# A hybrid decoder step on one core: the tokens in two groups, the second group's path laid between the expert gathers of the first

## The chip, the core and the metric

The kernel runs on one core of a Trainium2 chip. All tensors are 32-bit floats. The metric is the device time of one execution in microseconds (us). A core has five engines, each with its own instruction queue that is worked off strictly in order: TensorE (PE, matrix products into PSUM), VectorE (DVE), ScalarE (ACT), GpSimd (POOL) and SyncE (SP). Engines wait for each other through semaphores. DMA transfers are issued here by POOL (the "software" queue) and by SP (the "hardware" queue), and are carried by the core's 16 DMA engines.

## What is computed

One layer for 512 prompt tokens and 8 sample tokens of width 1024. Cut to what matters:

```python
ada = silu(c) @ w_ada + b_ada                      # six vectors of 1024 for the prompt, six for each sample
h = rmsnorm(x, g_pre_mix) * (1 + sc1) + sh1
aq, ak, av, conv_in, a_dec, b_beta, z, g_a, g_b = split(h @ w_in)
o_att = sliding-window attention (window 128, 8 heads, 2 key/value heads, sinks, relative bias)
conv_out = silu(4-tap causal convolution of conv_in)          # 1536 channels
o_d = gated delta rule over chunks (recurrent state, 4 heads of 128x128), RMS norm, gate silu(z)
merged = sigmoid(g_a) * (o_att @ w_att_out) + sigmoid(g_b) * (o_d @ w_delta_out)
x = x + gt1 * rmsnorm(merged @ w_out, g_post_mix)
h2 = rmsnorm(x, g_pre_ffn) * (1 + sc2) + sh2
# expert retrieval, for every token and each of 8 heads:
s = (h2 @ w_query) against 2 x 128 sub-keys;  16 best of each half, 16 best of their 256 sums
u, v = expert_u[eidx], expert_v[eidx]              # 16 experts a head, rows of 1024 each
f = sum over experts of softmax(best) * gelu(h2 . u) * v
x = x + gt2 * rmsnorm(f, g_post_ffn)
```

Besides x it returns the last keys and values, the last convolution inputs and the recurrent state of both token sets. Attention and delta rule look back only: a token needs the 128 keys before it, the 3 convolution inputs before it and the state left by earlier chunks.

## The kernel before, in words

**Two parts.** The first part (the "front") takes all 520 tokens through everything up to the scores. The second part is the expert retrieval. For tiles of 128 tokens (t = 0, 1, 2, the 8 samples as t = 4, then t = 3) and 8 heads (a "unit" is one tile and head) it gathers expert rows: one indirect DMA brings 128 rows of 8 KB (u and v side by side, 1 MB) into one of 7 ring slots. 4 gathers are a "quad", 4 quads a unit, 520 gathers in all.

**The loop per gather** (loops over QUADS on POOL, ACT, PE and DVE). POOL issues gather n (L338) when PE has freed slot n % 7 (ring_used). DVE takes the dot product of the slot's u half with the replicated tokens (L1427, dots_done). ACT applies gelu (L540) and scales the selection pattern S (L547, diag_ready). PE multiplies S with the v half, twice 512 columns, into fsum[0] and fsum[1] (L952 for tiles, L955 for the samples) and frees the slot. Before, each gather has its two products in turn: fsum[0], then fsum[1]. Between them DVE works on `search` for the unit two ahead, PE and ACT on `select` and, at the start of each tile, `replicate`. For t = 0 a quad also takes one block of w_query for tiles 1 to 3 and the samples (`query`).

**The front** in PE's order: 16 blocks of w_ada (`modulation`), transposes of x, 12 projections for the convolution, keys and values (wnat), 4 for the queries, 8 norms with projections between them, 4 attention blocks of 128 tokens with 3 projections each, the samples' attention, the delta rule (transposes, decay matrices, `lv` 1 to 6 of a triangular solve, recurrence over 4 chunks, the samples' step), 8 branch projections, `mix` with w_out for 5 tiles, `residual` on DVE, 16 query blocks for tile 0. `project` takes one 512 KB weight block with 8 products for each of two column parts (256 and 264 tokens). The profile records each 32-bit product as two entries. Almost all matrix products go through `mm` (L588). Weight blocks come on SP's queue in stream order into 4 or 5 places; SP waits for `w_used` of the block that held the place. POOL's queue carries all other loads and stores, and later the gathers.

**Order.** It is written out by hand, the same on every engine. PSUM: 4 banks that DVE empties (dbank), 2 that ACT empties (abank), 2 for fsum.

## Time and profile before

| | us |
|---|---|
| median of 3 runs | 2160.33 (2159.97 to 2164.02) |
| the profiled execution, its own time | 2168.11 |
| its span, first to last instruction | 2166.3 |
| first gather issued | 784.2 |
| mean granted TensorE clock | 0.940 of full |

| engine | busy us | share of the span |
|---|---|---|
| PE | 1681.8 | 78% |
| DVE | 1274.2 | 59% |
| ACT | 593.5 | 27% |
| POOL | 640.9 | 30% |

The profile is of one execution. Its page divides the span into 40 slices of some 54 us and shows each engine's busy share in tenths, the granted clock and the DMA traffic. The chain of waits is followed back from the last instruction. Shares over the whole span hide that the two parts have different limits, so the stretches before and after 784 us must be read apart.

### The profile page before, as it was taken

What the parts mean: (1) busy time and instruction counts of PE and PEld (TensorE: products, weight loads), DVE (VectorE), ACT (ScalarE), POOL (GpSimd) and SP (SyncE); (2) the same over time, 40 slices, a digit from 0 to 9 for tenths busy, and PEclk for the clock granted to TensorE, in tenths of its full rate; (3) what the DMA queues carried; (4) which work ended last, traced back from release to release, by engine and by line L of the source; (5) the groups of instructions that cost most, each with busy time, mean ns of one, the idle gap of its engine ahead of it and who ended that gap; (6) DMA issues with size and microseconds to landing.
All of it is one profiled execution on the core that took longest, in us unless ns stands there. A gap on an engine that the chain in (4) does not pass through costs nothing.

```text
span 2166.3 us, 22269 instructions
## 1 busy us (share of the span) xinstructions
PE 1681.8 (78%) x7458; PEld 810.0 (37%) x7458; DVE 1274.2 (59%) x2848; ACT 593.5 (27%) x1653; POOL 640.9 (30%) x596
## 2 busy tenths in 40 slices
PE   4999898979699988786776766776766777677776
PEld 1776677769676463332111111111111111111111
DVE  3441432177553655556666766767666767766754
ACT  1122344312100132223224223224223224332222
POOL 1001000000000024333544544544444543544542
PEclk9999999979789999998998999998999999899999
DMA  8336541000015179999999999999999998999997
GB/s 283 127 111 187 145 139 49 30 1 1 6 53 222 47 272 402 403 388 371 419 414 390 421 412 421 418 419 385 421 413 413 416 413 358 401 421 421 421 422 305
DMA packets 97954, 636.83 MB, mean 294 GB/s; under 512 B 11489, under 2 KB 11521, under 8 KB 30716
## 3 DMA queue, kind: packets, MB, share of 16 engines
q0 software_dynamic: 79248, 564.07, 64.4%
q1 hardware_dynamic: 18592, 71.34, 9.5%
q8 instruction: 59, 0.97, 0.2%
q14 instruction: 55, 0.45, 0.1%
HBM read 628.85 MB, written 7.56 MB: 294 GB/s over the span
## 4 chain that ended last, share of the span: by engine, by line
PE 43%; DMA 31%; ACT 10%; DVE 9%; issue 5%; another core or an unknown queue 1%; POOL 1%; ACTq 0%; DVEq 0%; SPq 0%; POOLq 0%
DMA arena<-in_euv,delta 28%; PE abank L588 18%; PE fsum L952 11%; PE dbank L588 9%; DVE arena L1427 3%; DMA arena<-in_wstream 2%; ACT delta L547 2%; ACT L492 1%; ACT L540 1%; ACT arena L352 1%; ACT small L540 1%; PE abank L905 1%; PE abank L891 1%; DVE arena L1174 1%
## 5 line engine op out<-in xcount | busy, mean ns | idle before, releaser
L952 PE MATMUL fsum<-arena,delta 128*32 128x512 f32 x2048 | 831.2, 673 | 369.3 <-ACT delta L547 367.4
L1427 DVE CUSTOM_DVE_ANT_0 arena<-arena 128x1024 f32<-128x1024 f32 x520 | 635.1, 1223 | 446.0 <-DMA arena<-in_euv,delta 430.7
L338 POOL DMA_INDIRECT arena<-in_euv,delta x520 | 595.7, 1146 | 735.4 <-PE fsum L952 648.2
L952 PEld LDWEIGHTS fsum<-arena,delta 128*32 128x32 f32 x2048 | 183.2, 118 | 970.5 <-ACT delta L547 669.0
L588 PE MATMUL abank<-arena 128*128 128x256 f32 (+5 forms) x2080 | 447.7, 375 | 23.0 <-DMA arena<-in_wstream 8.5
L588 PEld LDWEIGHTS abank<-arena 128*128 128x128 f32 (+2 forms) x2080 | 350.5, 191 | 122.1 <-issue 29.5
L540 ACT ACTIVATE small<-small 128x1 f32<-128x1 f32 x520 | 103.9, 200 | 641.3 <-DVE small L1427 627.9
L588 PE MATMUL dbank<-arena 128*128 128x128 f32 (+9 forms) x1072 | 225.9, 373 | 8.0 <-ACTq L461 2.9
L352 ACT ACTIVATE arena<-abank 128x512 f32<-128x512 f32 (+4 forms) x202 | 101.3, 501 | 415.1 <-PE abank L588 382.3
L588 PEld LDWEIGHTS dbank<-arena 128*128 128x128 f32 (+3 forms) x1072 | 165.1, 205 | 66.8 <-issue 50.1
L547 ACT ACTIVATE delta<-arena,small 128x32 f32<-128x32 f32 (+1 forms) x520 | 166.9, 321 | 17.2 <-ACT small L540 0.2
L309 POOL DMA_DIRECT2D out_deltap<-delta x1 | 0.6, 550 | 280.3 <-DVEq L1216 280.3
L1093 DVE RECIPROCAL arena<-arena 128x520 f32<-128x520 f32 x8 | 27.2, 3403 | 63.4 <-ACTq L408 63.4
L328 POOL CAST delta<-delta 128x16 uint32<-128x16 f32 x32 | 21.2, 662 | 131.1 <-ACTq L500 130.9
L623 PE MATMUL dbank<-arena,cT 128*9 128x256 f32 x384 | 34.6, 459 | 22.6 <-DMA arena<-in_wstream 16.3
L540 ACT ACT_TABLE_LOAD x35 | 44.9, 1283 | 0.8 <-ACT arena L352 0.2
L1427 DVE DVE_READ_ACCUMULATOR2_ANT small<- 128x1 f32 x520 | 42.7, 82 | 0.0
L492 ACT ACT_TABLE_LOAD x32 | 41.1, 1283 | 2.5 <-DVE arena L1360 0.6
L477 ACT ACTIVATE small<-small 128x1 f32<-128x1 f32 (+1 forms) x15 | 4.4, 294 | 129.7 <-DVE small L1283 129.6
L553 ACT ACTIVATE arena<-abank 128x384 f32<-128x384 f32 x16 | 7.9, 491 | 109.9 <-PE abank L588 109.9
L352 ACT ACTIVATE delta<-abank 128x32 f32<-128x32 f32 (+1 forms) x33 | 6.5, 197 | 113.6 <-PE abank L891 82.1
L905 PE MATMUL abank<-arena,consts 128*32 128x512 f32 x256 | 35.3, 602 | 1.8 <-ACT arena L352 1.8
(262 smaller groups left out, 1099.7 us busy)
## 6 DMA issues: line engine op xcount, KB each, us to landing
arena<-in_wstream SPq DMA_DIRECT2D x124, 512.0 KB, 4.6
arena<-in_euv,delta POOLq DMA_INDIRECT x520
arena<-in_x POOLq DMA_DIRECT2D x2, 2048.0 KB, 19.7
arena<-in_wout SPq DMA_DIRECT2D x1, 4096.0 KB, 17.3
arena<-in_sdel POOLq DMA_DIRECT2D x1, 2048.0 KB, 9.0
out_deltas<-arena POOLq DMA_DIRECT2D x1, 2048.0 KB, 8.7
arena<-mod POOLq DMA_DIRECT2D x4, 512.0 KB, 17.0
out_yp<-arena SPq DMA_DIRECT2D x4, 512.0 KB
```

Of the source, the lines that this page charges most:

```text
L338: pool.indirect_dma_start(ring[n % SLOTS], None, I["euv"], bass.IndirectOffsetOnAxis(cur[:, u % 2, c:c + 1], 0)).then_inc(ring_in[n % SLOT ...
L352: step(A(dst, src, func, **kw), s.aring_free)
L492: A(gexp[r, :], best[r, :], ACT.Exp, bias=nbest[r, :], accum_out=gsum[r, :]).then_inc(s.gexp_ready, 1)
L540: step(A(gel[:, q % 2, j:j + 1], dot[:, q % 2, j:j + 1], ACT.Gelu), s.gelu_done)
L547: A(S[:, q % 2, j, 0:wide], E4g[:, u % 2, c0:c0 + wide], ACT.Copy, scale=gel[:, q % 2, j:j + 1]).then_inc(s.diag_ready, 1)
L588: return pe.matmul(out, lhsT, rhs, start=first, stop=last)
L623: last = pe.matmul(mod_bank[0][32 * j:32 * j + NCOND, half * 256:half * 256 + 256], cT[:, at_, :], w[:, j * 256:(j + 1) * 256], start=at_ ...
L891: last = pe.matmul(b[32 * k:32 * k + 32, 8 * j:8 * j + 8], ident[:, 32 * j:32 * j + 32], pick[:, :, 4 * k:4 * k + 4], start=True, stop=Tru ...
L905: last = pe.matmul(b[32 * k:32 * k + 32, :], ident[:, 32 * j:32 * j + 32], h2[:, t, g * 512:(g + 1) * 512], start=True, stop=True, skip_gr ...
L952: last = pe.matmul(fsum[g][32 * j:32 * j + 32, :], S[:, q % 2, j, :], v, start=first_quad(q), stop=last_quad(q), skip_group_check=True)
L1093: step(recip(r, r))
L1427: TTR(uh, uh, rep[j] if t < NT else h2sb, 1.0, 0.0, ALU.mult, ALU.add, dot[:, q % 2, j:j + 1]).then_inc(s.dots_done, 1)
```

## The change

The tokens are cut in two groups: group 0 is tokens 0 to 255, group 1 is tokens 256 to 511 and the 8 samples. On PE, ACT and DVE the front becomes a Python generator `group(g)` that yields after each of many short segments, 281 in all (118 of group 0, 163 of group 1); a segment has the same number on all three engines. Before the retrieval starts, 110 segments are issued: all of group 0 up to its 9th of 16 query blocks. The retrieval is cut in "ticks" of 2 gathers (8 a unit, 4 for the samples), and after each tick the engine issues its segments up to a due number:

```diff
+SEGS_BEFORE = 110
+SEGS_ALL = 281
+PACE = 1.55
+def due(i):
+    if i < 0:
+        return SEGS_BEFORE
+    return min(SEGS_ALL, SEGS_BEFORE + int((i + 1) * PACE))
```

PE issues up to due(i) after tick i, ACT and DVE up to due(i - 1). So the 171 remaining segments lie in the first 111 or so of 260 ticks. Tile 2's search needs group 1's scores from tick 112 on.

The weight stream has the blocks of w_in after w_ada, the branches and w_query a second time (60 blocks of 512 KB), and w_out is loaded twice, in halves; group 1 has 4 places of its own:

```diff
+    order += list(range(QUERY, QUERY + 16))
+    first = len(order)
+    order += list(range(CONV, QUERY + 16))
...
+PLACE = [n % 5 if n < N_EARLY else 5 + (n - N_EARLY) % 4 for n in range(len(STREAM))]
```

`project` has one part (256 or 264 columns). Group 1's loads and stores (x, the caches, bias, the samples' state, w_out, the modulation rows) are issued by SP in between, each behind a wait; POOL has only gathers from the first one on. Group 1's w_out and weights share memory, so the second half of w_out waits for three results of the first, and the query weights for all six:

```diff
+            sp.wait_ge(s.merged_ready, N.merged_ready + KT)
+            sp.dma_start(wout[1][0], I["wout"][:, :, 0:512]).then_inc(s.wout_in, 16)
...
+            sp.wait_ge(s.mx_ready, N.mx_ready + 3)
+            sp.dma_start(wout[1][1], I["wout"][:, :, 512:D]).then_inc(s.wout_in, 16)
+            sp.wait_ge(s.mx_ready, N.mx_ready + 6)
```

Carried from group 0 to group 1: the last 3 convolution inputs (`carry`), the last 128 keys and values (`kvc`), the state (`delta`).

In the retrieval loop on PE the two gathers of a tick are taken together, first both into fsum[0], then both into fsum[1]; their S patterns have different groups of 32 output rows:

```diff
+                pair = [(n + e, (2 * (k % 2) + e)) for e in range(2)]
+                for e in range(2):
+                    for n_, j in pair:
+                        if e == 0:
+                            pe.wait_ge(s.diag_ready, n_ + 1)
+                        v = ring[n_ % SLOTS][:, D + 512 * e:D + 512 * e + 512]
...
+                            last = pe.matmul(fsum[e][32 * j:32 * j + 32, :], S[:, n_ // NQ % 2, j, :], v,
...
+                n += 2
+                if k == 0 and u + 1 < len(UNITS):
+                    select(u + 1)
...
+                work.until(due(i))
```

PSUM: 2 banks for `select` and `replicate` alone (fbank), 4 for the front (2 that DVE empties, 2 that ACT empties; group 0 borrows the fsum banks for DVE's). Group 0's solve has one gate projection a level, its recurrence two, each attention block two; group 1's 16 gate projections stand in a row after the samples' state. In the convolution ACT now makes the first tap, and DVE the other three as one instruction each for the prompt; the samples' taps are 8 instructions for all 12 blocks. `mix` goes to banks that ACT empties. The window copies of the caches are issued near the start.

## Rows read from the trace of the kernel before

**Rows 1.** The page's 40 slices, DMA busy share and rate.

```profile
DMA  8336541000015179999999999999999998999997
GB/s 283 127 111 187 145 139 49 30 1 1 6 53 222 47 272 402 403 388 371 419 414 390 421 412 421 418 419 385 421 413 413 416 413 358 401 421 421 421 422 305
```

**Rows 2.** Windows: busy us of PE, PEld, DVE, ACT, POOL; clock, DMA share, GB/s.

```profile
0.00:784.20 784.20, 690.02 (x3752) 533.11 (x3753) 357.85 (x631) 172.32 (x348) 23.53 (x44) 0.94 0.32 104
784.20:2166.30 1382.10, 991.74 (x3712) 276.94 (x3708) 916.39 (x2218) 421.14 (x1305) 617.42 (x552) 0.94 0.98 402
...
850.00:900.00 50.00, 40.81 (x205) 18.55 (x198) 30.27 (x78) 13.13 (x45) 20.08 (x19) 0.97 0.99 402
...
1900.00:1950.00 50.00, 36.60 (x114) 7.83 (x113) 34.86 (x87) 16.61 (x49) 24.46 (x22) 1.00 1.01 422
```

**Rows 3.** The gathers' line: duration ns min/median/max, starts; POOL's idle time before.

```profile
L338 POOL DMA_INDIRECT arena<-in_euv,delta x520: 939/947/4372, 784.2 to 2140.3; - x174
...
  PE fsum L952: 648.2, 310
```

**Rows 4.** Timeline: the first gather's dot; one gather of the steady part, DVE to PE.

```profile
789.84 1.23 DVE L1427 CUSTOM_DVE_ANT_0 arena<-arena 128x1024 f32<-128x1024 f32 x1 [3.79 <-DMA arena<-in_euv,delta]
...
1930.08 1.23 DVE L1427 CUSTOM_DVE_ANT_0 arena<-arena 128x1024 f32<-128x1024 f32 x1 [1.25 <-DMA arena<-in_euv,delta]
...
1931.34 0.20 ACT L540 ACTIVATE small<-small 128x1 f32<-128x1 f32 x1 [1.93 <-DVE small L1427]
1931.58 0.32 ACT L547 ACTIVATE delta<-arena,small 128x32 f32<-128x32 f32 x1
...
1931.95 1.91 PE L952 MATMUL fsum<-arena,delta 128*32 128x512 f32 x4 [0.58 <-ACT delta L547]
```

**Rows 5.** Chain that ended last: start us, us; a backlogged quad and a gather.

```profile
837.32 3.99 PE fsum L952 x16
...
1930.16 12.21 DMA arena<-in_euv,delta
```

**Rows 6.** The same chain through the front, where its stages begin.

```profile
54.95 8.97 PE abank L588 x32
...
149.84 25.31 PE abank L588 x112
...
204.56 7.27 PE abank L588 x32
...
213.63 19.65 DMA arena<-in_wstream
...
312.63 8.76 PE abank L588 x48
...
426.30 6.01 PE dbank L588 x34
...
480.77 1.16 PE abank L588 x8
...
547.20 1.17 PE abank L588 x8
...
589.12 14.22 PE dbank L588 x66
...
606.98 67.01 PE dbank L588 x272
...
675.30 69.03 PE dbank L588 x160
...
746.34 7.43 PE abank L588 x64
```

**Rows 7.** DMA issues: KB each, us from issue to landing.

```profile
skew<-bext POOLq DMA_DIRECT2D x1, 1536.0 KB, 37.0
```

**Rows 8.** Groups of instructions by line: busy us, mean ns, idle before.

```profile
L540 ACT ACT_TABLE_LOAD x35 | 44.9, 1283 | 0.8 <-ACT arena L352 0.2
L1093 DVE RECIPROCAL arena<-arena 128x520 f32<-128x520 f32 x8 | 27.2, 3403 | 63.4 <-ACTq L408 63.4
```

2303 lines of the change are left out of this document (1351 added, 952 removed).

## The prediction, made before the result was known

> **What bounds the kernel now.** I read the page's slices first. The DMA row is low and ragged up to slice 14 and stands at 9 from there to the end, at 370 to 422 GB/s [rows 1]. So there are two parts with different limits. The windows put numbers to them: from 0 to 784.2 us the DMA engines are busy 0.32 of the time and PE for 690 us; from 784.2 on DMA is busy 0.98 of 1382.1 us, PE 992, DVE 916 [rows 2]. The gathers' own line dates the border: 520 of them, first issued at 784.2, and POOL sits idle 648 us before them, released by PE freeing a slot [rows 3]. That could look like a bound by PE, but a gather takes 12.21 us from issue to landing [rows 5], and at 422 GB/s [rows 2] one MB takes 1.049/0.422 = 2.49 us, so some five are in flight: the slots are the limit on what is queued, DMA on the rate. The work on a landed gather is short: dot 1.23, gelu 0.20, S 0.32, products 1.91 us, about 3.8 us in all [rows 4]. 7 slots x 2.49 = 17.4 us is one round of the ring; without its DMA part 12.2 about 5 are left, and they are used. The second part is thus bound by bytes (545 MB of gathers / 0.422 = 1292 us of its 1382), the first by PE's order and the cross-engine chains.
>
> **The change, the part before the first gather.** Only group 0 goes ahead. A projection of all tokens takes 7.27 us [rows 6]; with 256 columns 3.6. Stage by stage, from the starts in [rows 6]: up to 54.95 nothing is per token, 55 us stay 55. Convolution 94.9 us for 12 blocks, 7.9 each, becomes 4.3 each: 51. Keys, values, queries 54.7: two tiles of five and four narrower projections: 29. Norms 108.1, with a 19.65 us wait for weights which falls together with the skewed write, 37.0 us to landing [rows 7], which stays: less 8 x 3.6 and a little, 75. Attention 113.7 for four blocks: two blocks and fewer projections in them, but the softmax chain stays whole: 50. Samples' attention and decay matrices 54.5: 20. Solve 66.4, 11.1 a level: half the DVE work, but a projection of 3.6 on PE is put in each level: 63. Recurrence 41.9: two chunks, two projections: 28. Samples' step 17.9: gone. Branches 68.3: 29. Mix 71.0: 4 of its 10 sums, 28, and the last tile's residual no longer hidden by mix, 12: 40. Queries 37.9: 9 blocks of 3.6, scores, search, select: 39. The sum is 479; I take a first gather at **480**, bounds 445 and 535 (the lower if the weight wait goes, the upper if norms and attention are chains and keep their length). Against 784.2 that is **-304 us** (-339 to -249).
>
> **The change, the bytes that come in.** While gathers run, group 1 brings 60 weight blocks (31.5 MB), 7 of group 0 (3.7), w_out 4.2, x twice 2.1, wnat 1.1, bias 1.0, caches 1.0, state in and out 4.2, modulation rows 1.6: 50.4 MB, where the kernel before had 16 blocks, 8.4 MB. 42 MB more at 0.402 to 0.422 [rows 2] is **+100 to +105 us, I take +103**. That a weight block costs no more than its bytes is shown at 850 to 900, where one block a quad came in at 0.99 DMA share [rows 2].
>
> **The change, what the weave costs beyond bytes.** 171 segments at 1.55 a tick are 110 ticks. Their DMA time is 110 x 4.97 = 547 plus 50.4/0.422 = 119: 666 us, 6.05 a tick. DVE's own retrieval work is 34.86 of 50 us [rows 2], 3.45 a tick, 381 us; group 1 adds about 175 (half of 357.85 [rows 2], less a convolution that is cut to three instructions, plus the samples): 556. PE: a lone gather costs 1.91 [rows 4], a backlogged one 3.99/4 = 1.0 [rows 5], since products of different gathers write different rows of a bank and overlap when they are neighbours in the queue; the new pairing makes them neighbours, so 220 x 1.0 = 220. Group 1's and group 0's last products are some 420: 67 projections of 3.6 are 240, mix 6 x 6.9 = 41 (69.03 for 10 [rows 6]), the rest is half of what 690 leaves. 640 in all. So PE and DVE both fit under 666 **on average**. They don't fit in each stage, and here I price what goes beyond the bytes. The rule: DVE does the segments one tick later than PE. Of two segments in a tick the second waits on PE for the first one's answer, which DVE gives only behind its next dots. For a stage with DVE work d a segment and an answer of p from PE and ACT, a tick is about 3.45 + 1.55 d + 0.55 p.
> - Solve, 14 segments, 9 ticks: DVE 4.3 a level (half the 8.6 or so of four chunks), then dots, ACT, PE: some 11 us a level or 8.4 a tick against 5.0: +31.
> - Residual of three tiles: 24 us DVE on top of 20 in 6 ticks, six roots that each need a table load of 1.28 [rows 8]: 53 against 29, +24.
> - Mix: 41 + 7 us PE in 4 ticks plus two waits for halves of w_out behind the gathers' traffic: +25.
> - Recurrence +19, decay matrices +15, norms (a reciprocal of half of 3.4 [rows 8] and a table load each) +15, attention +14 with the wait for bias, samples' attention and step +19, waits for x and state +10, the rest +10.
> Sum +182. A stall of up to 12.2 - 5.6 = 6.6 us costs nothing when five gathers are in flight (5.6 is the first gather, alone in the queue, from its issue at 784.2 [rows 3] to its dot at 789.84 [rows 4]), four or so times: -27. I take **+155**, bounds 0 (averages decide) and +300 (each of the 171 segments waits 1.75 us more, near the 1.91 of a lone product [rows 4]).
>
> More DVE work could also slow POOL. A gather's issue takes 947 ns in the median and 4372 at most [rows 3], so something blocks it at times. Of this SBUF — State Buffer of the Trainium skill (Who interferes with whom) says that GpSimd cannot write descriptors while DVE runs a copy or tensor_scalar in a two-port mode, while a tensor_tensor with two inputs does not stop it. Group 1's DVE work is nearly all of the second kind, so by the rule nothing is added; were it of the first, 1 us on each of 220 issues would still lie under the 3 us that a gather has.
>
> A table load shows 1283 ns, with 0.8 us of idle time before all 35 of a group [rows 8]. ScalarE: Activation LUTs of the Trainium skill (What ACT_TABLE_LOAD costs) counts a drain with each switch, 2.66 us in all. Some 30 visits to another table, there and back, are 77 us of ACT by the row and 160 by the skill; the sum goes by the row.
>
> **The sum.** Span 2166.3 - 304 + 103 + 155 = 2120. The profiled execution lies 1.8 above its span and 7.8 above the median of the runs: 2120 + 1.8 - 7.8 = **2114 us**. After tick 111 the parts are alike, and the end is the same.
>
> **Rivals.**
> 1. *The weave hides nearly everything* (mechanism: the ring's cushion and three engines that run a tick apart absorb the stage peaks; DMA stays at 9). For it: at 850 to 900 PE was at 40.81 of 50 us and DMA still at 0.99 [rows 2]. Against: that work had no chain in it. It costs 40 instead of 155: about 2000 us (1960 to 2050).
> 2. *The weave locks the engines in step*, and the gathers starve: place, the chain stages (norms to recurrence, mix, residual); each wait on PE holds back the products that free slots, POOL issues late, and after five landed gathers DMA runs dry. It decides from a loss of 304 - 103 = 201 us, or a tick of (666 + 201)/110 = 7.9 us. With 1.75 us more a segment the loss is 300: about 2260 (2170 to 2320). For it: PE has 640 of 666 us of work, so nothing of what it waits is given back, and POOL is released by PE in 648 us of its waits [rows 3]. Against: only some 100 segments have a chain.
> 3. *The front does not shrink as said*, since it is chains and not columns: first gather at 535, the rest as forecast: 2169, slower by a hair or the same.
>
> **Chances.** Forecast (2050 to 2165) 0.43, rival 1 0.26, rival 2 0.25, rival 3 0.06. The range that leaves out 2 in 10 reaches into both main rivals: 1985 to 2220. The cases of both signs hold much of the chance; the likeliest one's own range is 2050 to 2165. A measurement tells 0.2% (4.3 us) from no change. Faster by more: 0.26 + 0.39 = 0.65; within: 0.05; slower: 0.25 and parts of rival 3 and of the forecast's upper end, 0.30.
>
> **What the profile after would show.** Front: the first gather at 480, and 11 us a level of group 0's solve. Bytes: 42 MB more in all, DMA share 0.9 or less from 480 to about 1300 with dips at solve, mix and residual, 0.98 or more afterwards. Weave: the gather of tick 111 issued some 820 us after the first (666 + 155) against 547 by bytes alone; rival 1 has it at 710, rival 2 at 960. Pairing: products of a tick in about 2 us. If POOL's idle time is released by products that themselves waited for DVE or ACT in segments, rival 2's mechanism is at work. It would be wrong in size if loads on SP's queue landed late enough to hold PE for more than a few us each, or if PE's granted clock fell in its waits.

## The result, and the profile after it

The changed kernel takes **2242.24 us** (median of 4 runs, 2232.38 to 2246.39) beside 2160.47 for the kernel before: 1.0368 times as long, 95% interval 1.033 to 1.0407. It is slower by 3.7%. The forecast was 2114, faster, with 2220 as its upper end: wrong in sign, and outside its range. The profiled execution has a span of 2230.6 us.

The page's 40 slices of the kernel after, 56 us each, to be read beside [rows 1]:

```profile
PE   3968687879498668886698567966766666666664
DMA  7766023139799779684699557899999999999997
GB/s 270 236 168 221 19 73 126 57 103 356 285 375 351 275 295 354 236 302 192 265 377 369 206 216 272 348 412 394 407 421 421 421 420 367 377 421 421 421 421 301
```

Gathers run from the end of slice 9 on. Up to slice 26 the DMA row goes up and down between 4 and 9, and GB/s between 192 and 377; from slice 27 on both stand as they did before. The changed kernel has three parts: the front (up to the first gather), the weave (the stretch in which segments and gathers alternate, up to the gather of tick 111), and a rest that is like the old one. Windows of the kernel after (columns as in [rows 2]):

```profile
0.00:495.60 495.60, 373.44 (x2018) 282.07 (x2022) 163.18 (x296) 110.54 (x208) 13.11 (x26) 0.90 0.44 140
495.60:1438.90 943.30, 721.11 (x3485) 401.29 (x3478) 563.77 (x1278) 326.42 (x821) 251.33 (x235) 0.85 0.78 299
1438.90:2230.60 791.70, 506.67 (x1983) 109.32 (x1981) 527.01 (x1257) 242.05 (x744) 374.12 (x317) 0.94 0.97 400
```

And before, the stretch in which the same 222 gathers were issued, from the first one to that of tick 111:

```profile
784.20:1375.90 591.70, 436.14 (x1776) 145.16 (x1772) 383.71 (x946) 181.80 (x567) 258.85 (x235) 0.93 0.98 401
```

The gathers' own line after, and what ended POOL's idle time ahead of it, beside [rows 3]:

```profile
L358 POOL DMA_INDIRECT arena<-in_euv,arena x520: 939/947/1999, 495.6 to 2205.8; - x174
...
  PE fsum L1202: 968.4, 258
```

So the first gather comes 288.6 us sooner (784.2 to 495.6), the weave takes 351.6 us more (591.7 to 943.3), and the last 298 gathers keep their 2.57 us each. -288.6 + 351.6 = +63, which is the difference of the two profiled spans (64.3). All that is to be explained lies in those 943 us. On average no engine is full in them: PE is busy 721 us, DVE 564, DMA 0.78. The change would have paid below 591.7 + 288.6 = **880 us**.

What the weave looks like from near, in windows of 50 us: a stretch of projections, one with w_out, and one with the residual:

```profile
1100.00:1150.00 50.00, 50.00 (x249) 32.86 (x248) 19.49 (x43) 13.64 (x43) 14.30 (x15) 1.00 0.88 349
1250.00:1300.00 50.00, 35.93 (x130) 12.27 (x131) 2.62 (x10) 5.39 (x17) 5.67 (x6) 0.86 0.41 150
1300.00:1350.00 50.00, 19.52 (x49) 5.41 (x45) 33.11 (x59) 21.21 (x39) 13.39 (x11) 0.61 0.68 262
```

PE is full in the first, idle for 14 of 50 us in the second with DVE all but stopped, and idle for 30 in the third at a granted clock of 0.61. Each stage has another limit. The chain of waits names them. First a wait for the samples' x, then PE in front of the two halves of w_out (SP asks for each only when group 1 has come far enough; the profile names no releaser there and says "issue", and that it is w_out is shown by e5 below), then the residual:

```profile
554.58 12.79 DMA arena<-in_xs
...
1220.35 1.84 PE fsum L1202 x8
1222.19 15.84 issue
1238.03 16.34 PE bank L751 x32
...
1263.42 14.07 issue
1277.49 15.39 PE bank L751 x32
...
1316.11 1.28 ACT L601
...
1317.93 1.30 DVE arena L1703
1319.25 1.24 DVE arena L1704
...
1325.41 1.28 ACT L601
...
1327.23 1.30 DVE arena L1694
...
1334.70 1.28 ACT L601
```

The 1.28 us before each root (square root on ACT) is a table load, and the roots follow one another 9.3 us apart, one a tick: between them lie DVE's sums, two dots, another table load for gelu, S, and only then the next root.

To compare runs I use two numbers of each: the length of the weave (first gather to that of tick 111) and PE's busy time in it. PE's waits are the difference. And I divide the weave by stages, at the starts of the dots whose ticks carry them. "Forecast" is what the prediction listed for the stage beyond its average tick. In the changed kernel:

```text
stage of group 1              ticks     from-to, us      us a tick  over 6.05 a tick   forecast
x, norm, transposes           0-10      503.3-591.2        8.8        +27                +10 (x and state)
convolution to g/beta         10-26     591.2-707.8        7.3        +20   )
gates, branches               70-86    1066.0-1206.6       8.8        +44   )            +10 (the rest)
h2 transposes to scores       96-110   1344.9-1442.9       7.0        +13   )
norms                         26-32     707.8-765.8        9.7        +22                +15
attention                     32-42     765.8-837.8        7.2        +12                +14
decay matrices                47-51     866.5-895.0        7.1         +4                +15
solve                         51-59     895.0-960.1        8.1        +17                +31
recurrence                    59-64     960.1-997.9        7.6         +8                +19
samples' attention and step   42-47, 64-70                 8.8        +30                +19
mix and residual              86-96    1206.6-1344.9      13.8        +78                +49
sum                                                                  +275               +182
```

The borders are those of DVE, which runs ahead of PE, so a stage of PE can show late. This matters in the last row. DVE's dots of tick 91 start at 1237.0 us and those of tick 92 at 1303.6: before its first residual part DVE waits for all six sums of `mix`, and PE needs from 1222.2 to 1301.6 us for them, 29.9 us of it in the two waits. The six ticks with a root each (92 to 97) take 8.9, 9.3, 9.3, 13.8, 9.3 and 7.4 us, 58 in all, the fourth with a 3.67 us wait for modulation rows.

### The profile page after: what moved, and what is told of

Same layout as the page of the kernel before. It is cut to its first block, busy times and chain, and to the rows that moved or that the text cites. A ratio compares the mean times of both kernels' runs of the same rounds, so it can differ in the third digit from the quotient of the medians.

```text
span 2230.6 us, 22523 instructions
## 1 busy us (share of the span) xinstructions
PE 1601.2 (72%) x7480; PEld 792.7 (36%) x7480; DVE 1254.0 (56%) x2830; ACT 679.0 (30%) x1772; POOL 638.6 (29%) x578
## 2 busy tenths in 40 slices
DMA packets 112212, 667.87 MB, mean 299 GB/s; under 512 B 12353, under 2 KB 15953, under 8 KB 44972
## 4 chain that ended last, share of the span: by engine, by line
PE 39%; DMA 25%; DVE 18%; issue 9%; ACT 8%; DVEq 0%; SPq 0%; POOL 0%; ACTq 0%; POOLq 0%
PE bank L751 26%; DMA arena<-in_euv,arena 20%; PE fsum L1202 9%; DVE arena L1867 5%; DMA arena<-in_wstream 4%; PE fsum L751 1%; ACT arena L727 1%; ACT small L720 1%; PE fbank L1183 1%; DVE arena L1547 1%; PE bank L819 1%; DVE arena L1451 1%; ACT arena L387 1%; DVE arena L1563 1%; PE fsum L776 1%
## 5 line engine op out<-in xcount | busy, mean ns | idle before, releaser
L1202 PE MATMUL fsum<-arena 128*32 128x512 f32 x2048 | 725.8, 674 | 350.4 <-ACT arena L727 348.0
L358 POOL DMA_INDIRECT arena<-in_euv,arena x520 | 607.3, 1168 | 1086.1 <-PE fsum L1202 968.4
L751 PE MATMUL bank<-arena 128*128 128x264 f32 (+9 forms) x2960 | 679.2, 388 | 113.9 <-DMA arena<-in_wstream 31.5
L751 PEld LDWEIGHTS bank<-arena 128*128 128x128 f32 (+4 forms) x2960 | 520.1, 200 | 292.0 <-issue 132.7
L1202 PEld LDWEIGHTS fsum<-arena 128*32 128x32 f32 x2048 | 134.3, 116 | 846.7 <-ACT arena L727 632.3
L387 ACT ACTIVATE arena<-bank 128x512 f32<-128x512 f32 (+3 forms) x150 | 77.1, 514 | 419.0 <-PE bank L751 403.1
L727 ACT ACTIVATE arena<-arena,small 128x32 f32<-128x32 f32 (+1 forms) x520 | 166.9, 321 | 18.1 <-ACT small L720 0.6
L720 ACT ACT_TABLE_LOAD x59 | 75.7, 1283 | 66.2 <-DVE small L1867 64.1
L819 PE MATMUL bank<-consts,arena 128*128 128x128 f32 x176 | 32.7, 338 | 54.6 <-DVE arena L1479 29.3
L1402 DVE SCALAR_TENSOR_TENSOR arena<-arena,cols 128x256 f32<-128x256 f32 x72 | 35.1, 487 | 60.0 <-ACT arena L424 58.3
L1183 PE MATMUL fbank<-arena,consts 128*32 128x512 f32 x256 | 37.7, 652 | 5.0 <-ACT arena L672 5.0
## 6 DMA issues: line engine op xcount, KB each, us to landing
arena<-in_sdel SPq DMA_DIRECT2D x1, 2048.0 KB, 11.9
```

The source lines that it names most:

```text
L358: pool.indirect_dma_start(ring[n % SLOTS], None, I["euv"], bass.IndirectOffsetOnAxis(cur[:, u % 2, c:c + 1], 0)).then_inc(ring_in[n % SLOT ...
L387: step(A(dst, src, func, **kw), s.aring_free)
L720: step(A(gel[:, q % 2, j:j + 1], dot[:, q % 2, j:j + 1], ACT.Gelu), s.gelu_done)
L727: A(S[:, q % 2, j, 0:wide], E4g[:, u % 2, c0:c0 + wide], ACT.Copy, scale=gel[:, q % 2, j:j + 1]).then_inc(s.diag_ready, 1)
L751: return pe.matmul(out, lhsT, rhs, start=first, stop=last)
L819: last = pe.transpose(b[:, e * P:(e + 1) * P], src, ident)
```

## The experiments

All times are medians, each with the kernel before run beside it (2160 to 2168 us). "Weave" and "busy" are from the profiled execution.

```text
kernel                   time us   ratio to before (95%)       weave   PE busy   PE waits  clock  DMA
changed                  2242.24   1.0368 [1.033, 1.0407]       943     721       222      0.85   0.78
e1_unpaired              2237.76   1.0359 [1.034, 1.0377]       946     721       225      0.86   0.78
e3_pace3                 2350.18   1.087  [1.0852, 1.0889]     1057     766       291      0.85   0.69
e5_no_wout               2216.56   1.0239 [1.0216, 1.0262]      913     715       198      0.87   0.80
e6b_no_loads             2189.78   1.0102 [1.0078, 1.0127]      894     719       175      0.87   0.79
e7_no_sqrt               2231.14   1.0301 [1.0281, 1.0321]      941     721       219      0.86   0.78
e8_no_lag                2565.36   1.1832 [1.1801, 1.1863]     1258     832       426      0.80   0.60
e9_by_gather             2340.27   1.0802 [1.078, 1.0825]      1044     827       217      0.88   0.73
e10_dve_later            2229.12   1.0286 [1.0266, 1.0306]      928     716       212      0.85   0.79
e11_after_5places        2408.01   1.1111 [1.1088, 1.1134]      994     747       247      0.84   0.75
e12_few_bytes            2249.11   1.0384 [1.0363, 1.0405]      951     727       224      0.84   0.72
e13_two_ticks            2316.24   1.0678 [1.0648, 1.0708]     1024     744       280      0.83   0.73
e14_by_weight            2236.87   1.0327 [1.0304, 1.035]       938     726       212      0.87   0.79
e15_best                 2218.99   1.0239 [1.0213, 1.0265]      916     725       192      0.87   0.80
e16_half_projections     2217.19   1.0238 [1.0216, 1.026]       918     656       262      0.83   0.78
e17_half_products        2209.00   1.0198 [1.0179, 1.0216]      913     643       270      0.81   0.79
e18_all_three            2161.54   0.9978 [0.9962, 0.9994]      868     578       290      0.77   0.76
```

### The pairing (e1_unpaired, e2_before_paired)

```diff
-                for e in range(2):
-                    for n_, j in pair:
+                for n_, j in pair:
+                    for e in range(2):
```

> The changed kernel with one part undone: PE takes the two gathers of a tick one after the other again (fsum[0], fsum[1], then the next gather). If PE's own work is what fills the weave (640 of some 666 us by the prediction), a tick's products go from about 1.85 us to about 2.6 us where PE is behind, over 111 ticks 80 us, and the time rises to about 2320. If the weave is long because engines wait for each other and for loads, PE has idle time in most stages and only the projection stages (some 55 ticks) feel it: 20 to 45 us, about 2275.

> The kernel before with the pairing alone: in a quad the products of gathers 0 and 1 are taken together, then those of 2 and 3. DMA bounds its second part, so all theories expect little: 0 to -8 us, the gain only in tile 0 where queries load PE. A loss of up to 15 us would show that holding back a slot until its neighbour's pattern is there costs the ring more than PE gains.

e1 gives 2237.76 and the same weave; e2, the kernel before with pairs, 2168.01 us (ratio 1.0022, 1.0007 to 1.0037), no gain and perhaps a hair slower. Both of e1's expected values are missed: the order within a pair is without weight. It is another question whether two gathers side by side cost less than two set apart; e9 shows below that they do.

### What group 1's path costs by itself (e4_unwoven, e3_pace3)

e4 issues group 1's path up to segment 258 before the first gather:

```diff
-SEGS_BEFORE = 110
+SEGS_BEFORE = 258
...
-    if i < 0:
+    if i < 50:
         return SEGS_BEFORE
-    return min(SEGS_ALL, SEGS_BEFORE + int((i + 1) * PACE))
+    return min(SEGS_ALL, SEGS_BEFORE + int((i - 49) * PACE))
```

> The changed kernel with 258 segments before the first gather: all of group 1 up to its first query blocks runs without gathers in between, only the last 23 segments are woven in, from tick 50 on. It measures group 1's path alone. From group 0's own path (443 us from its convolution to the first gather) I expect 380 to 430 us for it, the first gather at 880 to 930, and about 2290 in all. What the weave hides is that length less the 350 us by which the woven ticks are longer than the same ticks before: 30 to 80 us. If contention between gathers and the weave's loads were the cause of the long ticks, the path alone would be short, 300 us, and this kernel would be faster than the woven one, near 2190.

2447.25 us, ratio 1.1329 [1.1305, 1.1352]. The window over what was put ahead, and the 222 gathers after it:

```profile
495.60:1062.70 567.10, 387.95 (x1801) 296.78 (x1803) 184.18 (x340) 104.42 (x226) 0.20 (x1) 0.80 0.23 75
1062.70:1656.00 593.30, 414.00 (x1756) 123.60 (x1748) 392.38 (x979) 187.88 (x573) 279.06 (x235) 0.93 0.98 400
```

This is the number that my forecast never worked out. Two groups one after the other take 1062.7 us to where one pass over all tokens took 784.2: 278.5 more. PE's busy time accounts for 76 of it (378 + 388 against 690), its idle time for the other 203: it goes with what comes twice, the chains, the table loads and the waits for transfers, which I haven't priced one by one. My expectation for e4, 380 to 430 us for this path, was far too low as well, and its rival, that gathers and loads hinder each other and the path alone is short (300 us), is refuted. What lies ahead of the gathers in e4 and not in the changed kernel is 567 us, PE busy in 388 of them: group 0's last queries and group 1's path up to the transposes of h2. The last 23 segments are woven from tick 50 on and cost nothing (593.3 for 222 gathers), as the 16 whole query blocks cost nothing in the kernel before. The weave hides 567 - 351.6 = 215 us of this, 38%. It would have had to hide 279.

e3 sets the rate to 3.0 segments a tick instead of 1.55, so that 57 ticks carry them.

> The changed kernel with a pace of 3.0 segments a tick instead of 1.55: the weave takes 57 ticks instead of 111. If every segment has a price of its own (chains through three engines, waits for loads), the weave's segments cost the same and fewer gathers are hidden under them: the 57 ticks take about 57 x 13 = 740 us, the other 54 then 280, 1020 against 943: about 2320. If the price is one of ticks (each handshake of a tick costs once) the time falls, to about 2150 to 2200. If bytes bound it, the sum of bytes is the same and the time stays at 2242.

The 57 ticks took 759 us, the weave 1057, the whole 2350.18: near the numbers expected of "each segment has its own price". Fewer ticks beside the segments hide less.

### Waits for group 1's loads (e5_no_wout, e6b_no_loads) and roots (e7_no_sqrt)

e5 leaves out both loads of w_out of group 1 and their waits, e6b also those of x, skew, caches, state and modulation rows:

```diff
-            sp.dma_start(wout[1][0], I["wout"][:, :, 0:512]).then_inc(s.wout_in, 16)
...
-            sp.dma_start(wout[1][1], I["wout"][:, :, 512:D]).then_inc(s.wout_in, 16)
```

> The changed kernel without the second group's two loads of w_out (2 x 2.1 MB): the mixing product of group 1 reads what already lies in those areas, so its values are not the reference's. In the changed kernel the tensor engine waits 15.84 us and 14.07 us for the two halves, each asked for by SP only after a step of group 1. Theory 'the lateness is made of waits for loads that are asked for too late': the two waits go, and nothing else moves in, 2197 to 2212 us (30 to 45 less than 2242). Rival 'it is the bytes': 4.2 MB at 421 GB/s are 10 us, 2232 us. Rival 'something else is late there anyway': 2242 us.

> The changed kernel without group 1's own loads of x, skew (the attention's bias), the samples' keys and values, the samples' state (sdel), w_out and the modulation rows: group 1 computes on what already lies in those places, so its values are not the reference's. The weight stream, the natural weights and the residual's x stay. Some 12 MB are not moved, 29 us of bytes. Theory 'waits for loads asked for at the last moment': the waits of 21 (x), 9.6 (skew), 11.9 (state), 15.8 and 14.1 us (w_out) and 3.7 (modulation) go, the time falls by 75 to 100 us to 2142 to 2167, which is the time before or a little under. Rival 'bytes alone': 2213. Rival 'the engines run in each other's step, waits for loads lie beside that': over 2213.

> The changed kernel with each of group 1's square roots on ScalarE (the norm of x, the norms of keys and queries, of the delta output, of the residual) replaced by a plain copy, which needs no other function table, so its values are not the reference's. 59 table loads took 75.7 us of ScalarE in all in the changed kernel. Theory 'handshakes between ScalarE and VectorE set the pace in the stages with roots' (norms 9.7 us per tick, residual 19.4 us per tick): each load of 1.28 us and what hangs on it goes, some 15 to 30 loads of group 1 in the chain, 2202 to 2222 us. Rival 'the roots lie beside other waits': within 5 us of 2242.

e5: 2216.56 us (26 less); the weave is 30.0 us shorter, which is just the two waits of 15.84 and 14.07. Ticks 90 to 95 go from 117 to 85 us, no other stage moves by more than 3. e6b: 2189.78, the weave 49.6 us shorter: 38 in ticks 90 to 95 (to 78), 10 in the stage of x, 5 in the samples' step, while others are a little longer. PE's waits fall by 47, its busy time by 2. So waits for loads that are asked for too late are real and add one for one, but they are 50 us and not the 75 to 100 that I expected; with them gone the kernel is still 1% slower than before. e7: 27 table loads fewer, 37 us less busy time of ACT. In the ticks with roots the loads are in the chain, and there their removal shows, 7.14 us from root to root where it was 9.30:

```profile
1324.01 0.10 ACT small L611
...
1331.15 0.10 ACT small L611
```

Over the whole weave the profiled execution is only 2.5 us shorter, since other stages took longer, attention above all (6.5 us). The median is 11 lower, with single runs from 2221.72 to 2242.28 beside 2232.38 to 2246.39. So the table loads are worth some 11 us at most, between the two expectations; outside the residual the roots lie mostly beside other waits.

### The bytes (e12_few_bytes)

```diff
+                if n >= N_FIRST:
+                    sp.dma_start(wplace[PLACE[n]][:, 0:P], I["wstream"][STREAM[n]][:, 0, :]).then_inc(w_full[PLACE[n]], 16)
```

> The changed kernel, but of each of group 1's 60 weight blocks only an eighth is loaded (the same 60 transfers, waits and products; what lies in the other seven eighths of a place is used as it is, so the values are not the reference's). 27.5 MB less, 65 us at 421 GB/s. Theory of the forecast, that a byte moved in the weave costs its time at the full rate: the time falls by 65 us, to 2177. Rival 'the queue stands idle a fifth of the weave, so the bytes lie in time that is lost anyway': under 25 us, 2217 to 2242.

2249.11 us, none of the 65. 27.5 MB less brought nothing at all: the DMA share of the weave fell from 0.78 to 0.72 and its length stayed.

```profile
498.00:1448.90 950.90, 726.68 (x3485) 404.87 (x3478) 563.60 (x1278) 326.00 (x821) 247.92 (x235) 0.84 0.72 268
```

For these bytes, 65 of the 103 us that the forecast charged, the price is thereby refuted; the other bytes were not taken out by themselves. In all stages but one the DMA share is 0.94 or less. The branches alone have 0.99, with PE busy 54.3 of 56.3 us, and e12 did not shorten them either.

### The order of the engines (e8_no_lag, e10_dve_later, e11_after_5places)

In the changed kernel ACT and DVE take a tick's segments one tick after PE. e8 takes this away, e10 adds half a tick for DVE:

```diff
-                work.until(due(i - 1))
+                work.until(due(i))
...
-                work.until(due(i - 1))
+                work.until(due(i))
```

> The changed kernel, but ScalarE and VectorE take group 1's segments of a tick in the same tick as the tensor engine does, not one tick later. Theory 'each engine's part of a stage waits a whole tick for its turn': where a stage of group 1 is a ping-pong between engines it gets shorter by up to a tick in some 15 places, 2140 to 2200 us. Rival 'the lag is what lets the engines run past each other': without it ScalarE and VectorE stand waiting for the tensor engine's results ahead of the dots of group 0, slower, 2260 to 2320 us. I hold the second for likelier (0.6).

> The changed kernel, but VectorE takes group 1's segments of tick i after the first of the two dots of tick i+2, half a tick later than in the changed kernel; ScalarE stays one tick behind. Theory 'more lag, more slack between the engines' (no lag at all cost 323 us): faster, 2190 to 2225 us. Rival 'the tensor engine now waits longer for VectorE inside a tick, with the next gathers' products behind the wait': slower, 2260 to 2320 us. Even odds.

e8 gave the largest change of the study: 2565.36 us, 323 more, well past what either theory had. PE's waits, first the kernel after, then e8 (PE line, what it waited for: us, times, longest):

```profile
PE fsum L1202 <- ACT arena L727: 81.2, 24, 17.0
PE bank L751 <- issue: 29.9, 2, 15.8
PE bank L751 <- DMA arena<-in_wstream: 14.9, 1, 14.9
```

```profile
PE fsum L1202 <- ACT arena L727: 378.9, 108, 15.4
```

Without the lag the products of nearly every tick wait for ACT's S. The chain of e8 in group 1's solve shows one such tick from end to end:

```profile
1100.06 1.11 issue
1101.17 0.10 DVE small L1867
1101.29 0.21 ACT small L720
1101.53 0.33 ACT arena L727
1101.86 0.04 issue
1101.90 4.13 PE fsum L1202 x8
1106.03 3.89 PE bank L751 x32
1109.96 0.04 issue
1110.01 0.70 DVE arena L1563
```

Dot, gelu, S, products, group 1's products, group 1's DVE work, dot: one after the other, two pipelines made into one chain. This is engines in each other's step in its pure form; the lag of a tick saves 315 of the weave's us. Of these, 204 are waits of PE and 111 are busy time for the same work: the granted clock of the weave was 0.80 in e8 against 0.85, and the 8 entries of the chain above take 4.13 us at a granted clock of 0.59 where the changed kernel had 1.84 at 1.00. With half a tick more for DVE the weave is another 15 shorter (e10, 2229.12 us, ratio 1.0286, outside both of its expected ranges), PE's waits for S 62 us instead of 81; the ticks with roots go from 9.3 to 6.9 us, the norms' from 9.7 to 8.0, while solve, attention and queries get longer by 0.5 to 1.0.

> The changed kernel with 5 places for gathered rows instead of 7. A gather takes 12.2 us to land and some 4 us more to be used, so where nothing else holds it up 5 places give one per 3.2 us instead of 2.58: the stretch after the weave grows from 767 to about 960 us. The weave has 4.25 us per gather. Theory 'the weave is limited by group 1's chains and loads': it grows by under 20 us, since 16.2 us / 4.25 us are under 4 places. Rival 'a late segment is made up out of the places that wait filled': with fewer of them the weave grows by 100 us or more.

2408.01 us. The stretch after the weave took 894 us for its 298 gathers (3.0 each; 960 expected). The weave grew by 51, between the two numbers: slack in the ring helps there, but its limit is elsewhere.

### The grain of the weave (e9_by_gather, e13_two_ticks, e14_by_weight, e15_best)

e9 weaves after each gather instead of after two, with ACT and DVE two gathers behind, e13 after each fourth (cuts from PE's loop):

```diff
+                            if n_ % 2 == 0:
+                                work.until(due2(n_))
```

```diff
-                work.until(due(i))
+                if i % 2 == 1:
+                    work.until(due(i))
```

> The changed kernel, woven by the gather instead of by the tick: after each gather's product the tensor engine takes 0 or 1 segment of group 1 (0.775 on average; by the tick it was 1 or 2), and ScalarE and VectorE take theirs two gathers behind it, which is the same lag. Same segments, same total. Taking the lag away cost 323 us, so the order in the tick has weight. Theory 'the engines run in each other's step, a tick at a time': in smaller portions a gather's product is held up by one segment rather than two, and the weave shrinks by 30 to 80 us, 2160 to 2210 us in all. Rival 'it is the segments' own chains': the same 2242 within 8 us.

> The changed kernel, woven by two ticks: the tensor engine issues group 1's segments only after every second tick, 3 or 4 at once, ScalarE and VectorE one tick later. Four gathers' products stand next to each other. Theory 'the tensor engine's own work is the limit, and products that stand alone cost nearly twice' (272 us for 216 gathers' products in the weave, 379 us when woven by the gather, with 100 us more in the time): products at 1.0 us a gather, 216 to 225 us in the weave, some 50 us less, 2180 to 2205 us in all. Rival 'the chains of group 1 weigh more': three dependent segments in a portion each wait a hand-over, so the chain stages (norms, attention, residual) grow as the products shrink, 2240 to 2320 us. I give the first 0.45.

Both went the other way: e9 2340.27 us, e13 2316.24. e9's reason stands in its chain, here in the stage of gates:

```profile
1183.67 1.83 PE fsum L1209 x4
1185.50 3.76 PE bank L758 x16
```

4 entries, one gather, take 1.83 us; in the changed kernel 8 entries, two gathers, take 1.84 (the chain above, at 1220.35). The products of two gathers go to different groups of 32 rows and run together if they are neighbours in the queue. Apart they cost PE double where PE is full; over the weave it is busy 105 us more and the weave is 100 longer. PE's lines over the weave, gathers' products only, the kernel after and e9 (busy us, mean ns, then idle before):

```profile
L1202 PE MATMUL fsum<-arena 128*32 128x512 f32 x864 | 271.7, 696 | 82.5 <-ACT arena L727 81.2 <-ACT arena L387 0.7
```

```profile
L1209 PE MATMUL fsum<-arena 128*32 128x512 f32 x864 | 379.0, 665 | 125.6 <-ACT arena L734 125.5
```

e13 had the reverse: its products did not get cheaper (294 us), and PE waited 170 us for S instead of 81. My reading, for which I show no chain: with three or four of group 1's segments in a row, each needing an answer that DVE and ACT give only after their next dots, PE comes late to the next tick. My theory for e13, that joining four gathers makes their products cheaper and the time shorter, fell here. One tick is the best of the three grains.

e14 gives stages of projections 2.1 to 2.6 segments a tick, chain stages 0.8 to 1.35:

```diff
-    return min(SEGS_ALL, SEGS_BEFORE + int((i + 1) * PACE))
+    at = float(SEGS_BEFORE)
+    for _ in range(i + 1):
+        at += next((r for end, r in RATES if at < end - 1e-6), 1.0)
+    return min(SEGS_ALL, int(at + 1e-6))
```

> The changed kernel with another rate of segments a tick, stage by stage, the same 171 segments in the same 110 ticks: 2.1 to 2.6 a tick in the stages that are projections (convolution, gates, branches, queries), 0.8 to 1.35 in the chain stages (norms, attention, solve, recurrence, mix, residual), where the changed kernel has 1.55 throughout. Theory 'PE-bound stages add, chain-bound stages hide': a gather's product costs PE 1.26 us where PE is the limit and nothing where it waits for others; some 25 ticks are moved from the first kind to the second, 2 x 1.26 us each, 2160 to 2200 us in all for 45 to 80 us, of which at least 40 I expect. Rival 'each segment and each tick has its price wherever it stands': 2242 within 10.

> As e14_by_weight, with VectorE half a tick later (that alone gave 13 us) and group 1's x loaded into the free area of the convolution as soon as group 0's branches are summed, ahead of the gathers, not behind the scores (VectorE waited 21 us for it). If the three add, 13 + 12 us below e14_by_weight: 2140 to 2180, about the time of the kernel before. If the waits of the chain stages overlap, under 10 us below e14_by_weight.

e14 2236.87: nothing, as its rival said. Its waits for S rose to 95 us as others fell. e15, with x loaded early and DVE half a tick later, 2218.99: 18 below e14, somewhat less than the 25 if all added, and the best version with the whole computation, still 2.4% slower than before.

### Taking work from PE (e16_half_projections, e17_half_products, e18_all_three)

```diff
-                    for k in range(KT):
-                        last = mm(b[:, 0:W], w[:, k, :], x[:, k, :], k == 0, k == KT - 1)
+                    few = KT // 2 if g else KT
+                    for k in range(few):
+                        last = mm(b[:, 0:W], w[:, k, :], x[:, k, :], k == 0, k == few - 1)
```

```diff
-                for e in range(2):
+                for e in range(1 if t < 2 else 2):
                     for n_, j in pair:
```

> The changed kernel with each of group 1's 52 projections (convolution, queries of attention, z, gates, w_query) summed over 4 of its 8 parts of the width, so that its values are not the reference's. Same weight blocks, waits and results in number. 52 x 4 x 0.46 us = 95 us less work of PE, 7 us of it or so where PE waits for others in any case. Theory 'PE's own work is what the weave is made of': 60 to 95 us less, 2147 to 2182 us. Rival 'the chains and the gathers' bytes take over as soon as PE is relieved': DMA has 547 + 119 us of the weave's 943, and the projections' stages run at 7.1 to 8.5 us a tick against 5.0 to 6.1 by bytes, so at least a part comes; under 45 us less, above 2197.

> The changed kernel without the second of the two products of each gather for tiles 0 and 1 (the upper 512 columns of their retrieval sum are not made; 256 gathers, of which 222 lie in the weave). 111 to 136 us less work of PE in the weave, all of it in the gathers' part of a tick. Theory 'PE's own work adds one for one': 90 to 136 us less, 2106 to 2152 us, less than the kernel before. Rival 'the products lie mostly in the time in which a tick waits for its S pattern and group 1's answers': under 60 us less, above 2182.

> e12_few_bytes, e16_half_projections and e17_half_products in one kernel: an eighth of each of group 1's weight blocks is loaded, its projections are summed over half of the width, and tiles 0 and 1 have one product a gather, so the values are not the reference's. The three alone moved the time by +7, -25 and -33 us. Theory 'limits close to one another, each hiding the relief of the other': clearly more than their sum of 51, 100 to 150 us less, 2090 to 2140 us. Rival 'the hand-overs between the engines, one tick apart, are a floor': the sum or less, 30 to 60 us less, 2180 to 2212 us. The first 0.5; in the stages of projections alone (316 us of the weave) the tick could fall from 7.5 to some 5.5 us, 80 us in all.

e16 takes 65 us from PE's busy time and 25 from the weave; e17 78 and 31. The remaining 40 and 48 come back as waits. So PE's work is a limit in part of the weave and no more. e18, both and the small weight blocks, shortens the weave by 75 us where the three alone gave 25 + 31 - 8 = 48, and the time by 81, between the two expected ranges: there are limits close to one another that hide each other's relief, but much of the time belongs to none of the three. The windows of e16, e17 and e18:

```profile
494.10:1412.40 918.30, 656.13 (x3090) 333.86 (x3083) 560.08 (x1271) 325.08 (x819) 248.47 (x236) 0.83 0.78 303
```

```profile
498.90:1411.40 912.50, 642.72 (x3053) 386.57 (x3046) 562.17 (x1276) 325.00 (x820) 249.06 (x235) 0.81 0.79 308
```

```profile
494.20:1362.30 868.10, 577.70 (x2659) 316.67 (x2652) 559.62 (x1272) 324.20 (x818) 253.32 (x236) 0.77 0.76 290
```

The table by stage says which part moves (us a tick, first dot to first dot):

```text
                   ticks   changed   e12    e16    e17    e18
norms              26-31     9.7    10.9    9.7   10.0    9.5
solve              51-59     8.1     8.2    8.2    8.0    8.0
mix and residual   90-96    19.4    19.6   19.9   19.6   19.7
convolution        10-18     8.5     8.6    7.9    8.1    7.6
gates              70-80     8.4     8.2    8.4    8.2    6.9
branches           81-86     9.7     9.8    8.2    8.0    7.7
queries            98-109    7.1     7.1    6.4    6.6    5.2
```

Norms and solve don't move, whatever is taken from PE or from the bytes. Nor does the third row, but it is no evidence of a chain: none of the three takes anything from `mix` or from its waits for w_out, which fill most of it. The stages of projections move most when all three go. In the gates, e16 alone gave nothing: PE is busy 62.4 us there against 65.8 in the changed kernel, at a mean clock of 0.79 against 0.84, and idle 21.4 against 18.5. A late weight block stands in this stage of all five kernels (14.9 us in the changed one, 12.4 in e12, where a block has an eighth of its bytes): in the changed kernel SP asks for it only at 1082.48, right behind the store of the samples' state at 1082.09. e6b left this load in place. In e16 the chain goes through it:

```profile
1077.31 12.38 DMA arena<-in_wstream
1089.68 0.04 issue
1089.73 3.89 PE bank L751 x8
1093.62 2.30 PE fsum L1203 x8
1095.91 1.98 PE bank L751 x8
```

A block that is late by 12.38 us, and behind the wait the same 8 entries take 3.89 us where they take 1.98 once PE has worked again: half the speed, at the lower of the clock's two levels. The window over the 3.89 us has a granted clock of 0.50:

```profile
1089.70:1093.60 3.90, 3.87 (x10) 2.58 (x12) 0.00 (x0) 0.00 (x0) 0.00 (x0) 0.50 0.73 239
```

This goes with the small yield of relieving PE. In the weave the mean clock is 0.85 in the changed kernel, then 0.83, 0.81 and 0.77 in e16, e17 and e18. As an estimate from busy time times clock, e18 has 168 us of work at full clock less (721 x 0.85 against 578 x 0.77), but PE is busy only 143 less. Even with a fifth of PE's busy time gone the kernel is level with the one before (0.9978).

## Why the prediction was wrong, step by step

**What bounds the kernel before.** Right, as far as the rest of the gathers shows: 400 GB/s and 2.57 us a gather, before and after.

**The front.** Right. First gather at 495.6 against 480 (bounds 445 to 535), -288.6 against -304. A level of group 0's solve takes 10.37 us (starts 302.91, 313.28) where about 11 were forecast:

```profile
302.91 4.61 PE bank L751 x24
307.52 1.80 PE fsum L751 x16
...
313.28 4.61 PE bank L751 x24
```

The other terms of its sum were not compared one by one, so some of the agreement can be errors that cancel.

**The bytes.** The amount was right: the weave moved 943.3 x 0.299 = 282 MB, 222 gathers are 233, so 49 beside them (forecast 50.4). "42 MB more in all" was not: the whole kernel moves 667.87 MB against 636.83, 31 more, and the rest had left the front. The price was wrong: 103 us forecast, and the 27.5 MB of e12, 65 us by that price, were worth nothing in a weave whose DMA share is 0.78. I had myself forecast a weave that is slower than its bytes.

**The weave beyond the bytes.** This is the step that failed. In the sum of the forecast the weave was 591.7 + 103 + 155 = 850 us and it is 943, 93 more; the front adds 15.6, together 109 of the 111 us by which the span differs (2120 to 2230.6). By the forecast's own rate of 6.05 us a tick the stages exceed by 275 where it listed 182 and took off 27, which is 120 too little and not 93: the forecast priced the stages over 666 us but added the price to 591.7 + 103 = 695 (its two values for tick 111, 820 in its signs and 850 in its sum, are these two bases). The table by stage shows which lines. Solve, recurrence, decay and attention were forecast too high, 79 where they are 41. The others were too low: projections by 67, mix and residual by 29, x by 17, the samples by 11, norms by 7. Projections were "the rest, +10" and are +77, over 46 ticks that take 355 us. Half of this is PE's own work: it is busy 316 us where 6.05 a tick are 278. I had looked at PE on average over the weave (640 of 666 us), but there the projections stand in rows, and a tick with 1.55 projections of 3.70 us and the products' 1.84 is 7.6 us of PE. The other half, 39 us, is idle time of PE, with waits for S and the one late weight block (14.9 us) in it. Mix with the residual is +78 against 49. The sums of `mix` with the gathers' products between them took PE about what I said (49.5 us without the waits, 48 forecast), and so did the six ticks with roots (58 us, 3.67 of it a wait for modulation rows, against 53). What the sum lacked is the two waits for w_out: its +25 for mix is 48 us less four average ticks, which leaves them about 1 us, and they are 29.9. I had named SP's issue order and put next to nothing for it. The 27 us taken off for the ring's cushion can't be told apart in these runs; e11 shows only that with two slots fewer the weave is 51 us longer.

**PE's work.** 640 us were forecast, 721 measured. Products in pairs cost 1.84 a tick where they stand in the chain, as said, but 1.26 us a gather in the mean over the weave (271.7 us / 216) where I put 1.0. By busy time times clock the two nearly agree, so the difference goes with the lower clock: it was 0.94 in the kernel before, from whose rows I took durations, and 0.85 in the weave, 640 x 0.94 = 602 against 721 x 0.85 = 613. The prediction names a fall of the clock in PE's waits as what would make it wrong in size, and puts no number to it.

**Rival 2, engines in step.** The result is its outcome: tick 111 at +943 us (it said 960; the forecast 820), a tick of 8.5 us (it decides from 7.9), a time near its 2260. Its mechanism is shown by e8 to work in this kernel, and by e10 to be still there with the lag. It is not the whole: projections that fill PE and loads asked for late (50 us, e6b) have each their share, and the largest stage that the rival names, mix, was late by its loads. So its time came out right in part by other means than its own. It deserved more than 0.25, and what told so was in reach. "DVE does the segments one tick later" was in my rule, but I summed it over the stages that I took for chains and let averages speak for all others.

**What I never worked out** is the price of two groups by themselves. The forecast's own numbers give it: 480 for group 0, of which the first 55 are not repeated, so 425 for group 1, before its samples and its waits for loads. e4 measured 567. The forecast's weave was 258 us over that of before; it thus claimed, unsaid, that 309 of 567 would be hidden. 215 were, and 279 were needed.

**POOL.** The rule weighed in the prediction (DVE's two-input operations do not stop GpSimd's descriptor writing) is not contradicted: an issue takes 947 ns in the median as before, 1999 at most against 4372, though DVE's busy share of the weave is 0.60. The mean of all is 1168 ns against 1146 before.

**Table loads** are the 1283 ns of [rows 8] here too. The drain that the Trainium skill adds to each in ScalarE: Activation LUTs (What ACT_TABLE_LOAD costs) is not seen: ACT's instruction before the load below ends at 1316.09, and the root starts 0.01 us behind it. Of the two loads a tick that e7 removes among the roots, 2.56 us by the rows, 2.2 came back.

```profile
1316.11 1.28 ACT L601 ACT_TABLE_LOAD   x1
1317.40 0.29 ACT L601 ACTIVATE small<-small 128x1 f32<-128x1 f32 x1
```

**What stays open.** Norms (9.5 to 10.9 us a tick) and solve (8.0 to 8.2) stay as they are when PE or the queue is relieved, and which hand-over sets them isn't shown; only among the roots were single links changed (e7 and e10). The kernel with group 1's loads asked for early, DVE half a tick later and less work on PE at once wasn't run, so how the limits add up beyond e15 and e18 is not known. More lag than e10's for all engines wasn't tried. Why e14 gave nothing, though its ticks moved where they should be free, is argued from its waits for S only.

## What to carry to other kernels

Before weaving a second pass into the gathers of the first, cost the pass by itself: what comes twice (chains, loads, table switches, stores) has to be hidden before the first microsecond is gained (here 279 of 567 us, and 215 were). An average over the weave says nothing of it, since each stage has another limit; price a tick of each stage by its fullest engine and by its chain, and take the larger. When two pipelines share in-order engines, the lag between the engines and the size of a portion are the first things to measure (here +315 us without lag, +100 with smaller and +80 with larger portions), and a load of the second pass must not be asked for where its result is next in line.

## What the runs showed of the hardware

- The products of two gathers into different groups of 32 rows take 1.84 us together, and those of one alone 1.83 us. The order within the pair is of no weight (e1), being neighbours in PE's queue is (e9). That products into different tiles of 32 columns run at the same time is what TensorE: Matmul & The Clock Gate of the Trainium skill says (Part 3: Packing small matmuls); these traces agree, with nearly the full factor of two for a pair.
- After a wait of 12.38 us PE went on at half of its speed: 3.89 us for 8 entries at a granted clock of 0.50, and 1.98 later (e16). The residual's 50 us had a granted clock of 0.61. With work taken from PE the mean clock of the weave was 0.83, 0.81 and 0.77 instead of 0.85 (e16, e17, e18), so relief gave less than the durations say.
- Single loads under the gathers' traffic can be late: the samples' state (2 MB) took 11.9 us from issue to landing against 9.0 in the kernel before, and PE waited up to 13.7 us for a weight block (0.5 MB) in e16; the median of all 168 blocks of the changed kernel is 5.4, that of the 124 before 4.6.
- 27.5 MB less in a stretch with a DMA share of 0.78 changed its length by +8 us; the changed kernel's own runs spread over 14 (2232 to 2246).
- A table load is 1.28 us of ACT with 0.02 us or less on either side (at 1316.11 in the changed kernel).
